# Attention on one core: a new order of TensorE's blocks, another split of banks, and a scaling with two operands

## The reference, cut to what matters

```python
s = einsum('qd,kd->qk', q, k) * scale + bias        # causal, 128 queries x 128*(i+1) keys
p = softmax(s)                                      # in local attention also times a gate
o = einsum('qk,kd->qd', p, v)
```

## Time and profile before

| what | value |
|---|---|
| median of 3 runs | 1412.79 us (1411.73 to 1414.3) |
| the profiled execution | 1421.27 us |
| its span, first to last instruction | 1419.7 us |
| TensorE busy | 1337.3 us, 94% |
| VectorE, ScalarE, GpSimd busy | 569.3, 339.1, 507.0 us |
| mean granted TensorE clock | 0.979 |
| fox, local, MLA (from the first scores) | 105.3 to 149.1, 221.5 to 312.4, 929.4 to 978.1 us |

### The profile page before, as it was taken

How to read it: one execution, slowest core, us unless ns; L and a number is a source line. 1 busy time by engine, 2 the same in 40 slices (tenths; PEclk the granted TensorE clock), 3 DMA queues, 4 the chain that set the end, 5 groups by cost and what they waited for, 6 DMA issues and landing times. The chain is left out here.

```text
span 1419.7 us, 24033 instructions
## 1 busy us (share of the span) xinstructions
PE 1337.3 (94%) x10076; PEld 807.4 (57%) x10076; DVE 569.3 (40%) x1381; ACT 339.1 (24%) x788; POOL 507.0 (36%) x586
## 2 busy tenths in 40 slices
PE   6998999899999979999999979998999999999997
PEld 5875444688888445434444424456777445655543
DVE  4355223671415262321211143462379571443415
ACT  2216124641010110011111123362211301322221
POOL 7668605666453800222222212065250012111062
PEclk9999999999999979999999999999999999999999
DMA  8290013401131586999999952011040431300131
GB/s 266 95 367 27 1 61 90 181 5 60 60 118 60 181 304 226 367 324 376 382 377 377 382 211 75 8 60 60 31 147 30 120 95 33 128 2 18 61 118 60
DMA packets 99793, 210.96 MB, mean 149 GB/s; under 512 B 14614, under 2 KB 22641, under 8 KB 99553
## 3 DMA queue, kind: packets, MB, share of 16 engines
q1 hardware_dynamic: 87152, 171.39, 34.0%
q0 software_dynamic: 12528, 37.97, 7.9%
HBM read 188.88 MB, written 19.42 MB: 147 GB/s over the span
## 5 line engine op out<-in xcount | busy, mean ns | idle before, releaser
L1579 POOL TENSOR_TENSOR AR<-Wt,AR 128x512 f32<-128x512 f32 x68 | 88.6, 1323 | 97.2 <-PE pb L1778 92.8
L3918 PE MATMUL pb<-Wt,HT 128*128 128x512 f32 x256 | 119.5, 609 | 1.0 <-DVE AR L4009 1.0
L818 POOL TENSOR_SCALAR AR<-AR,SM 128x384 f32<-128x384 f32 (+2 forms) x64 | 67.9, 1078 | 66.4 <-DVE SM L774 66.4
L2466 PE MATMUL pb<-AR 128*64 128x512 f32 x256 | 85.0, 595 | 0.7 <-issue 0.7
L2673 POOL DMA_DIRECT2D ys<-AR x28 | 15.1, 544 | 193.2 <-ACT AR L2637 193.2
L797 ACT ACTIVATE AR<-AR,SM 128x512 f32<-128x512 f32 (+3 forms) x128 | 70.5, 551 | 49.8 <-DVE SM L765 49.6
L765 DVE CUSTOM_DVE_ANT_0 AR<-pb,AR 128x512 f32<-128x512 f32 (+3 forms) x128 | 56.1, 486 | 55.6 <-PE pb L726 55.6
L3918 PEld LDWEIGHTS pb<-Wt,HT 128*128 128x128 f32 x256 | 46.8, 192 | 53.3 <-issue 49.8
L1778 PE MATMUL pb<-AR 128*128 128x256 f32 x320 | 73.2, 380 | 1.9 <-DVE AR L1985 1.2
L2466 PE MATMUL pb<-Wt,AR 128*64 128x512 f32 x192 | 70.8, 595 | 0.0
L1579 POOL TENSOR_TENSOR AR<-Wt 128x512 f32<-128x512 f32 x34 | 44.2, 1321 | 67.5 <-DMA Wt<-in_w_in_dram 31.1
(11 more groups left out here) (581 smaller groups left out, 2561.9 us busy)
## 6 DMA issues: line engine op xcount, KB each, us to landing
Wt<-in_w_in_dram SPq DMA_DIRECT2D x18, 2048.0 KB, 8.6
AR<-in_w_gate_dram SPq DMA_DIRECT2D x8, 2048.0 KB, 18.0
AR<-in_w_up_dram SPq DMA_DIRECT2D x8, 2048.0 KB, 19.3
AR<-in_w_down_dram SPq DMA_DIRECT2D x8, 2048.0 KB, 17.6
Wt<-in_w_gate_dram SPq DMA_DIRECT2D x6, 2048.0 KB, 18.1
Wt<-in_w_down_dram SPq DMA_DIRECT2D x6, 2048.0 KB, 14.8
Wt<-in_w_up_dram SPq DMA_DIRECT2D x6, 2048.0 KB, 21.1
ys<-AR POOLq DMA_DIRECT2D x2, 3072.0 KB, 25.7
```

The lines of the kernel that those rows point to most:

```text
L818: r = gt.tensor_scalar(s, s, w, None, ALU.mult)
L1579: r = gt.tensor_tensor(out[:, k:k + s, :], a[:, k:k + s, :], b[:, k:k + s, :], op)
L2466: r = mm(s[o:o + 64, :], XT[b % 2][:, k, 0:64], W.ap((n, b))[:, k, :], start=k == 0, stop=k == 7)
L3918: r = mm(s, HT[:, k, t * 128:(t + 1) * 128], W.ap(("gate2", c, br))[:, k, :], start=k == 0, stop=k == 7)
```

## The change

`there_and_back` replaces `steps` in `Attend`. In even steps TensorE goes scores (group n), turn (n - 3), values (n - 5); in odd steps values, turn, scores. VectorE's even step is score, inverse of n - 1, turn, inverse of n, ended of n - 5; its odd step is ended, turn, score. ScalarE's even step is score, turn and its odd step turn, score. Values come one step later, so `pT` has three buffers instead of two. Scores take their banks from a ring of four (0 to 3), turns from a ring of two (4 and 5); the other users keep S and T. L818 multiplies by a second operand, a column of ones. In the first block, the score tiles lie in X, the tile of x, which is loaded again behind `s_loc`; in MLA the third buffer lies in the weights' slot `uqkv`. The rest of the diff waits for the second load of x.

```diff
+def there_and_back(items, there, back):
+    for step in range(len(items) + 5):
+        for stage, behind in (back if step % 2 else there):
+            if 0 <= step - behind < len(items):
+                stage(items[step - behind])
+        yield 1
...
-        P = Psum(banks, {"S": (0, 1, 2), "T": (3, 4, 5), "O": (6, 7)},
+        P = Psum(banks, {"S": (0, 1, 2), "T": (3, 4, 5), "O": (6, 7), "scores": (0, 1, 2, 3), "turns": (4, 5)},
...
-                    s = [P.take(pe, "S", ("s", n, hp)) for hp in range(2)]
+                    s = [P.take(pe, "scores", ("s", n, hp)) for hp in range(2)]
...
-                        s = P.take(pe, "T", ("t", n, hp))
+                        s = P.take(pe, "turns", ("t", n, hp))
...
-                                       self.pT[n % 2][hp][:, off + j * 128:off + j * 128 + 128], start=begins and j == 0,
+                                       self.pT[n % 3][hp][:, off + j * 128:off + j * 128 + 128], start=begins and j == 0,
...
-                yield from steps(self.groups, score, None, None, turn, value)
+                yield from there_and_back(self.groups, ((score, 0), (turn, 3), (value, 5)), ((value, 5), (turn, 3), (score, 0)))
...
-                yield from steps(self.groups, score, inverse, None, turn, ended)
+                yield from there_and_back(self.groups, ((score, 0), (inverse, 1), (turn, 3), (inverse, 0), (ended, 5)),
+                                          ((ended, 5), (turn, 3), (score, 0)))
...
-                yield from steps(self.groups, score, None, None, turn)
+                yield from there_and_back(self.groups, ((score, 0), (turn, 3)), ((turn, 3), (score, 0)))
...
-                            r = gt.tensor_scalar(s, s, w, None, ALU.mult)
+                            r = gt.tensor_scalar(s, s, w, C["ones"][:, 0:1], ALU.mult, ALU.mult)
...
-        ar = Place(AR, ARN, 15872)
-        sc3 = ar.take(512)
-        att_sc = [[ar.take(512) for _ in range(2)] for _ in range(3)]
-        att_pT = [[ar.take(512) for _ in range(2)] for _ in range(2)]
-        att_sc.append([sc3, ar.take(512)])
+        ar = Place(flat(X[:, :, :]), 4096)
+        att_sc = [[ar.take(512) for _ in range(2)] for _ in range(4)]
+        ar = Place(AR, ARN, 16384)
+        att_pT = [[ar.take(512) for _ in range(2)] for _ in range(3)]
...
+            for t in ALLT:
+                ve.wait_ge(s_x[t], 32)
...
+        ar = Place(flat(W.ap("uqkv")), 2560, 1536)
+        att2_pT.append([ar.take(512) for _ in range(2)])
...
                     sy.wait_ge(s_loc, 1)
+                    for t in ALLT:
+                        nc.sync.dma_start(X[:, t, :], a["x"][0, t * 128:(t + 1) * 128, :]).then_inc(s_x[t], 16)
```

More of the change, by code:

```diff
@@ L778, in turn @@
                     ve.wait_ge(*P.filled(("t", n, 0)))
-                    vt.tensor_copy(self.pT[n % 2][0], P.ap(("t", n, 0))).then_inc(P.free(("t", n, 0)), 1)
+                    vt.tensor_copy(self.pT[n % 3][0], P.ap(("t", n, 0))).then_inc(P.free(("t", n, 0)), 1)
                 def ended(x):
@@ L803, in turn @@
                     ac.wait_ge(*P.filled(("t", n, 1)))
-                    st.copy(self.pT[n % 2][1], P.ap(("t", n, 1))).then_inc(P.free(("t", n, 1)), 1)
-                yield from steps(self.groups, score, None, None, turn)
+                    st.copy(self.pT[n % 3][1], P.ap(("t", n, 1))).then_inc(P.free(("t", n, 1)), 1)
+                yield from there_and_back(self.groups, ((score, 0), (turn, 3)), ((turn, 3), (score, 0)))
             def norm_po(self, x, gate=None):
@@ L2130, in ffn_norm_po @@
             out7.left_po(mixT, 2)
+            for t in ALLT:
+                po.wait_ge(s_x[t], 32)
             for i in range(2):
```

## The result

The changed kernel takes 1420.19 us (median of 20 runs) beside 1414.89 us for the kernel before (20 runs): ratio 1.0033, 95% interval 1.0019 to 1.0047. It is slower by 0.33%, between 2.7 and 6.7 us. The forecast was +2.0 us on the median then known (1414.8, range 1407 to 1424). The profiled execution took 1416.43 us, span 1415.1; it is a single one and less than the 1421.27 of the kernel before, so the two spans do not rank the kernels. The stages inside the spans can be compared, local to some 4 us only (see e8).

What follows compares the result with a forecast made beforehand. TensorE is busy 94% of the span; GpSimd's scaling sets fox and MLA's second half. Fox -3.1, local +9.5, MLA -6.4 and clock +2.0 give +2.0 us on the 1412.79 us median: 1414.8 us, range 1407 to 1424.

Steps and rivals of the forecast that it cites:

- GpSimd bound fox and MLA: Fox and MLA's second half: GpSimd's scaling takes 3.7 us a two-member group; two operands cut it to 1.6 to 2.3.
- The loop through ScalarE's turn copy: All stages: turn copy waits behind two groups' exponentials; a double step takes 7.18 us in fox, 7.65 in MLA.
- Output banks: Values 4 wait for VectorE's emptying, 1.1 us more in fox and MLA; values 8 wait 1.4 us in each stage.
- Sizes: Stage changes summed block by block: fox -3.1 us, local +9.5 us, MLA -6.4 us.
- The 2 us set apart for the clock: TensorE after waits: three more low-clock spells at 0.7 us, +2 us, bounds 0 and +9.
- the cause given for local: Local: six two-member double steps each lose 0.96 us through ScalarE's loop, 5.8 us of the +9.5 us.
- the shared banks: Local: compressed keys' turn holds ScalarE's turn bank, second products take scores 9's bank pair; "some of" the delay, unsized.
- The shape changes: TensorE: going there and back removes one change of matmul form a step, 0.18 us; 5 us over 40 steps.
- Waits half as long: Rival, chance 0.17: local loses only 4.7 us and the clock is unchanged; -4.8 us in all, 1408.
- TensorE sets all three: Rival, chance 0.10: ScalarE's copy is not late; fox -12, MLA -11.5, local -2.5, together -26 us, 1387.
- Scaling no faster: Rival, chance 0.07: two operands don't speed the scaling, fox and MLA gain nothing; +13.5 us, 1426.
- Low clock: Rival, chance 0.18: TensorE falls to its low clock in the holes, six more spells; +9 instead of +2, 1422.

Runs made afterwards that it cites:

- e8: The changed kernel with the one-operand scaling put back: 1431.79 us, ratio 1.0117 to the kernel before.
- e2: The kernel before with nothing but the two-operand scaling at L818: 1396.86 us, ratio 0.9875.
- e1: The changed kernel, but local attention keeps the old order, the old rings and values one step earlier: 1405.01 us, ratio 0.9934 to the kernel before.
- e4: The changed kernel, but in even steps ScalarE copies the turn of group n - 3 before group n's exponentials: 1419.82 us, ratio 1.0046 to the kernel before.
- e6: The changed kernel, but VectorE takes an even group's reciprocal in the next odd step, behind the turn's copy: ratio 0.9987 to the kernel before.
- e5: The changed kernel, but in even steps VectorE empties the output bank ahead of its own group's reciprocal: ratio 1.0028 to the kernel before.
- e7: The kernel before with the two-operand scaling and the rings of four and two banks, in the old order: ratio 0.9937.
- e10: The kernel before with two-operand scaling everywhere and the new rings in fox and MLA alone; local keeps old order and rings: 1393.64 us, ratio 0.9873.
- e12: The changed kernel, but the compressed attention also takes its banks from the rings of four and two: ratio 1.0038 to the kernel before.
- e11: The kernel before with two-operand scaling and new rings, old order, the compressed attention also taking its banks from these rings: ratio 0.9893.

## Why the prediction was right, and where it was off

- **Direction and size.** +2.0 us forecast, +4.7 measured (2.7 to 6.7): inside the range, and the signs of all three stages came as told. The largest term, local, came near by luck, as told below.
- **GpSimd bound fox and MLA, and the second operand frees it.** Right: 765, 662 and 449 ns where 778, 665 and 471 were taken, and e2 and e8 show the gain from both sides.
- **The loop through ScalarE's turn copy.** Right in MLA: scores 5 to 7 took 7.64 us (948.39 to 956.03) against 7.65, with the wait for L813 in its row, and the next double step, with values 4 in it, 8.86 against 8.8. Right in fox too: 7.19 us at the full clock (e1) against 7.18, and the turn starts 0.14 us after ScalarE's copy. In the kernel after it is 8.14 us, since the two scores were issued at the low clock (1.5 us more than at 127.15). e4 takes the loop away: 5.99 us. One remark there was wrong: the prediction says that no row of the old order has such a wait, but in local of the kernel before two turns wait for L804, 0.8 us in all.
- **Output banks.** Right in fox and MLA. Values 4 waited 2.16 and 1.37 us, and the double step with them took 8.25 us in fox (127.15 to 135.40) against 8.2. With the wait cut to 0.79 us (e6) it took 7.2. Values 8 waited 1.39 us in both (1.4). In local they waited 3.17 us, and that was not in the schedule.
- **Sizes.** Fox -1.9 instead of -3.1, for the low clock: e1's fox, without it, is 3.0 us shorter than before. MLA -6.6 instead of -6.4; local +11.0 instead of +9.5; the 0.9 us ahead of local was not foreseen. The 2 us set apart for the clock don't show in the profiled execution: MLA gained clock (0.96 to 1.00), fox too (0.92 to 0.96), local lost little. In the medians they may be there: the mean granted clock is 0.9833 over the 20 executions of the kernel after, and 0.9836 to 0.9850 in the three series of the kernel before. Times TensorE's 1337 us that is 0.4 to 2.3 us, an estimate.
- **The step that failed is the cause given for local.** The forecast made 5.8 of the 9.5 us of six double steps at 0.96 us through ScalarE's loop, with the shared banks "some of it". Scores 13 and 19 do come near it (at 56.6 us into the stage for 56.3, and 86.8 for 84.6). But no wait of TensorE in local names L813, and e4 takes the loop away with no less idle time (19.5 us beside 17.9); e5 and e6 take VectorE's waits away, with at most 1.1 us; and e7 shows 12.5 us from the rings alone. What stands in its place, of 17.9 us idle, are 3.2 us for the output bank, 4.2 us of the compressed attention for score banks, 3.7 us of turns with L829 in the bracket (1.7 in e2), and smaller waits. The sum was near by a wrong attribution, which is luck.
- **The shape changes.** Two scores in a row take 1.93 us to the next block (127.15 to 129.08) instead of 2 x 1.02 to 1.06: 0.11 to 0.19 us saved, where 0.18 was taken. The Trainium skill's rule that a change of tiling mode drains TensorE ("TensorEngine Tiling (Array Packing)", Tiling Modes) agrees with that row. The rival built on it fell all the same: the order that saves the changes pays more in waits.
- **The rivals.** "Waits half as long" fell: local has +11.0 us, not +4.7. "TensorE sets all three" fell for this order, but its stage lengths (fox about 31.8, MLA 37.2, local 88.4) are near what e10 reaches with the old order: 34.2, 38.9, 90.6. "Scaling no faster" fell. "Low clock" came in spells, in e8 (with the local of the kernel after) to 0.92 over the whole of local; its +9 us were not reached.

**Open.** Which wait of the new order holds local at 101 to 104 us: not ScalarE's loop, not VectorE's reciprocal, not the rings, each taken away by itself. In e12, with shared counters, the idle 18.9 us are spread over many waits, the largest 4.4 us in three. Untried are the fifth step of lag, the two value blocks in a row with one output bank behind them, and two of these at once. What made the clock low in local of e4 and e8 (0.92) isn't settled, nor are the 1 to 4 us between sum and measurement.

## What to carry to other kernels

Take a bundled change apart before judging any part: one line of it was worth -17.7 us, and the rest took all of it back and more. Where several users draw on the same banks, give them one counter, or banks of their own: in the old order this was worth 9.5 us of a stage (e11), in the new one nothing (e12), since another cause was enough by itself. An order that puts equal blocks next to each other doubles the bursts that the other engines' queues see; count the banks and the in-order waits for bursts, not for the mean rate. And where a bracket names an engine, look whether that engine had long done the part that is waited for.

## What the runs showed that was not expected

A GpSimd scaling of a 128x512 tile takes 1561 ns with one operand and 765 ns with two, in the same stage of two kernels that differ in nothing else (e8 and after); this is its row in fox of e8:

```profile
L827 POOL TENSOR_SCALAR X<-X,SM 128x512 f32<-128x512 f32 x8 | 12.4, 1561 | 16.4 <-DVE SM L782 16.4
```

The clock falls in short spells, and in the kernel after one of them comes right behind two waits. Windows of fox in the kernel after, around the two late turns (idle 1.17 and 0.71 us) and behind them:

```profile
117.00:119.00 2.00, 1.28 (x8) 0.82 (x8) 0.76 (x2) 1.21 (x5) 2.00 (x3) 0.94 0.00 0
119.00:122.50 3.50, 3.50 (x18) 2.17 (x17) 1.38 (x7) 1.16 (x3) 3.49 (x6) 0.55 0.00 0
122.50:127.10 4.60, 4.06 (x50) 3.39 (x48) 3.07 (x14) 3.94 (x17) 2.79 (x6) 1.00 0.00 2
```

TensorE is fully busy in the second stretch, and the granted clock is 0.55, near the lower of its two levels, 1.2 and 2.4 GHz; in the third it is back. But the waits alone don't bring it. e1 and e12 have the same two waits in fox (1.17 and 0.71 us), and the two scores behind them take 2.01 and 2.00 us, at the full clock; e5 has them too, and there the scores take 3.59 us. So with the same program in fox the clock falls in one execution and not in another, and stage lengths of single executions differ with it. e10, whose waits in fox after the first turn are 0.27 to 0.59 us each, shows 1.00 in all three stages. What decides it, no run here shows.
